# A two-layer boundary worked token tile by token tile: the last and the first four weight chunks, with norms, x pieces and transposes per tile

## The reference

```
y = sgu_mixer(h, ...)                          # ends with y @ w_out, K = 4096, N = 2048
x = x + gate * rms_norm(y, post_g[0])          # gate, scale, shift = cond @ ada_w + ada_b
h = rms_norm(x, pre_g[1]) * (1 + scale) + shift
cq, ckv, k_rope, z = jnp.split(h @ w_in, [448, 960, 1024], axis=-1)    # K = 2048
```

## Time and profile before

| | |
|---|---|
| median of three executions | 2643.91 us |
| profiled execution: time, span | 2648.92 us, 2647.1 us |
| mean granted clock of PE | 0.977 |
| PE busy | 2538.8 us (96%) |
| DVE busy | 1631.3 us (62%) |
| ACT busy | 1349.1 us (51%) |
| POOL busy | 424.9 us (16%) |
| DMA | 548.91 MB, mean 207 GB/s |

### The profile page before, as it was taken

One profiled execution on the slowest core, in us unless ns is written; L12 is line 12 of the kernel. 1 busy time (PEld: TensorE's weight loads), 2 busy tenths in 40 slices (PEclk: granted clock), 3 DMA queues, 4 the chain that ended last, 5 costly groups with the idle time before them and its releaser, 6 DMA issues.

```text
span 2647.1 us, 33773 instructions
## 1 busy us (share of the span) xinstructions
PE 2538.8 (96%) x11958; PEld 2098.1 (79%) x11958; DVE 1631.3 (62%) x2456; ACT 1349.1 (51%) x1845; POOL 424.9 (16%) x296
## 2 busy tenths in 40 slices
PE   4999999999996999997999999999999999999998
PEld 4788788888885888886778777878888888888887
DVE  7789887667765677755755555545555545545553
ACT  4555664444444455544467666644544444444443
POOL 0155463110020000010000000024110011110111
PEclk8999999999997999997999999989999999999999
DMA  9979877888773666653454545445555555565554
GB/s 345 331 264 341 272 250 256 273 286 282 250 272 110 202 203 203 211 184 110 154 167 152 174 153 165 149 153 179 187 191 191 185 195 184 185 195 183 185 184 140
DMA packets 363660, 548.91 MB, mean 207 GB/s; under 512 B 32300, under 2 KB 125840, under 8 KB 363152
## 3 DMA queue, kind: packets, MB, share of 16 engines
q1 hardware_dynamic: 361856, 541.37, 62.3%
q10 hardware_dynamic: 1680, 5.91, 0.6%
HBM read 545.13 MB, written 2.10 MB: 207 GB/s over the span
## 4 chain that ended last, share of the span: by engine, by line
PE 65%; DVE 2%; ACT 1%; issue 1%; POOL 0%; ACTq 0%; DVEq 0%; POOLq 0%
PE ps L1599 38%; PE ps L1604 19%; PE ps L1584 1%; PE ps L1586 1%; PE ps L1585 1%; PE ps L1827 1%; PE ps L1675 1%; PE ps L1826 1%; PE ps L1661 0%; PE ps L1649 0%; DVE tf L976 0%; DVE stage L1328 0%; PE ps L1927 0%; ACT hi L414 0%; PE ps L1926 0%
## 5 line engine op out<-in xcount | busy, mean ns | idle before, releaser
L868 DVE TENSOR_TENSOR lo<-raw,hi 128x1024 fp32r<-128x1024 f32 x838 | 1083.0, 1304 | 797.5 <-ACT hi L414 796.6
L414 ACT ACTIVATE hi<-raw 128x1024 fp32r<-128x1024 f32 x838 | 880.4, 1059 | 805.6 <-PE ps L1604 703.5
L1599 PE MATMUL ps<-hi,a_hi 128*128 128x512 f32 (+1 forms) x2208 | 877.2, 398 | 11.5 <-issue 4.7
L1599 PE MATMUL ps<-hi,a_lo 128*128 128x512 f32 (+1 forms) x2208 | 862.3, 391 | 0.0
L1604 PE MATMUL ps<-lo,a_hi 128*128 128x512 f32 (+1 forms) x2208 | 590.2, 390 | 3.0 <-DVE lo L868 3.0
L1599 PEld LDWEIGHTS ps<-hi,a_hi 128*128 128x128 f32 x2208 | 419.5, 190 | 102.0 <-issue 12.3
L1604 PEld LDWEIGHTS ps<-lo,a_hi 128*128 128x128 f32 x2208 | 415.5, 189 | 90.7 <-DVE lo L868 4.2
L1599 PEld LDWEIGHTS ps<-hi,a_lo 128*128 128x128 f32 x2208 | 419.6, 190 | 81.4
L1599 PE MATMUL ps<-hi,b_hi 128*128 128x512 f32 x1056 | 417.2, 395 | 1.7 <-DVE b_lo L952 1.4
L1599 PE MATMUL ps<-hi,b_lo 128*128 128x512 f32 x1056 | 412.7, 391 | 0.0
L1604 PE MATMUL ps<-lo,b_hi 128*128 128x512 f32 x1056 | 283.1, 390 | 0.0
(11 more groups left out here) (260 smaller groups left out, 1753.0 us busy)
## 6 DMA issues: line engine op xcount, KB each, us to landing
raw<-in_ada_w SPq DMA_DIRECT2D x96, 1024.0 KB
raw<-in_sgu_w_in SPq DMA_DIRECT2D x96, 1024.0 KB
raw<-in_w_up SPq DMA_DIRECT2D x64, 1024.0 KB
raw<-in_w_down SPq DMA_DIRECT2D x64, 1024.0 KB
raw<-in_w_in SPq DMA_DIRECT2D x42, 1024.0 KB
raw<-in_sgu_w_out SPq DMA_DIRECT2D x32, 1024.0 KB
raw<-in_w_in SPq DMA_DIRECT2D x128, 256.0 KB
raw<-in_mla_w_in SPq DMA_DIRECT2D x33, 512.0 KB
```

The source lines that it names most:

```text
L414: nc.scalar.activation(hi[:, q % CHUNKS, :], raw[:, r % RAWS, q % 2 * CW:(q % 2 + 1) * CW], ACT.Copy).then_inc(hi_ready, 1)
L868: nc.vector.tensor_tensor(lo[:, q % CHUNKS, :], raw[:, r % RAWS, q % 2 * CW:(q % 2 + 1) * CW], hi[:, q % CHUNKS, :].bitcast(F32), ALU.subt ...
L1599: nc.tensor.matmul(ps[:, 2 * s + t, 0:width], x[:, k0 + j, t * P:(t + 1) * P], hi[:, c, w], start=begins, stop=False)
```

## The change

In the second half of the last product the loop over blocks is written out. The fourth block's first-half sums are not copied to `y`: they stay in PSUM banks 2 and 3 (`stays`, `evicted=3`), and its second half is added to them there. The second of the four blocks uses banks 4 and 5 for that (`block_in(2)`). The fourth block's last four chunks are multiplied for tile 0 alone (24 matmuls), then for tile 1 alone (24 matmuls); `half_done` tells that tile 0 is complete, and the chunks count as used only as tile 1 is worked. The small matmuls of the conditioning vector stand behind them.

ACT squares the fourth block from PSUM, tile by tile (`act_tile_square`), and DVE multiplies it by the gate row (`dve_tile_gated`); POOL has three blocks instead of four. Each tile has its own two norms (`dve_tile_ss`, `act_tile_root`, `dve_tile_rstd`). x is updated, squared and scaled in pieces of 512 columns (`dve_x_update`, `act_x_square`, `dve_x_normal`). A transpose group is now four 128-column slices of one tile (`pe_quad`), taken in the order `QUADS`; scale and shift are on ACT, four instructions of 128 columns per group (`act_quad`), the remainder on DVE (`dve_quad`). In the second layer's first block, the first four chunks are multiplied for tile 0, then for tile 1, with the groups' transposes between them, and the last four for both. One root of a column of ones (`early`) stands before the fourth block, so that ACT's function table is loaded there. The core of the diff:

```diff
-            act_pairs_squared(act, n, None, y, raws=12)
-            act_root(act, n)
-            act_squares(act, n, lambda t: x[:, t, :], 0)
-            act_root(act, n)
-            act_split(act, n, 8, a_hi, modulated=True)
-
-            act_steps(act, n, 8)
...
+            nc.scalar.activation(early[:, :], ones[:, :], ACT.Sqrt)
+            act_steps(act, n, 5)
+
+            act.wait_ge(stage_free, n.stg.at(2))
+            act.wait_ge(half_done, 1)
+            act_tile_square(act, n, 0, 1)
+            act_tile_root(act, n, 0)
+            act_steps(act, n, 1)
+            for b in range(4):
+                act_x_square(act, n, 0, b, b + 1)
+            act.wait_ge(chunk_used, n.chunk.base + 2 + CHUNKS)
+            act_tile_square(act, n, 1, 1)
...
+            for i in range(2, 8):
+                act_quad(act, n, i, *QUADS[i], 1)
+                if i >= 4:
+                    act_steps(act, n, 1)
...
+        def act_quad(act, n, i, t, b, layer):
+
+            act.wait_ge(t_turned, n.tg.base + 1)
...
+                    ins = nc.scalar.activation(tf[:, i % 2, e * P:(e + 1) * P], bank, ACT.Identity,
+                                               bias=mod[:, layer, k:k + 1], scale=hscale[:, k:k + 1])
...
+                act.wait_ge(t_kept, n.kept.base)
+                ins = nc.scalar.activation(a_hi[:, 4 * b:4 * b + 4, to], tf[:, i % 2, :].rearrange("p (k s) -> p k s", k=4), ACT.Copy)
...
-            layer_out(dve, n, 0)
-            norm_x(dve, n)
-            layer_in(dve, n, 1)
+            dve_steps(dve, n, 5, ada=True)
+
+            n.bsq.base += 7
+            dve.wait_ge(block_sq, 2 + n.bsq.base)
+            dve_tile_ss(dve, n, 0, bss)
+            dve_tile_gated(dve, 0, 1, 2)
+            dve_tile_rstd(dve, n, 0)
...
+            for b in range(4):
...
+                dve_x_update(dve, 0, b)
+            dve_steps(dve, n, 1)
...
+            for i in range(2, 8):
+                dve_x_normal(dve, *QUADS[i])
+                if i >= 3:
+                    dve_quad(dve, n, i - 1, *QUADS[i - 1], 1)
+                    if i >= 5:
+                        dve_steps(dve, n, 1)
...
+QUADS = ((0, 0), (0, 1), (1, 0), (1, 1), (0, 2), (1, 2), (0, 3), (1, 3))
...
-            pe_pairs(pe, n, A, 2, ada=True, gate=True)
-            pe.wait_ge(n_out, 4)
-            pe_turn(pe, n, 8, cols(y), modulated=True)
...
+            for c in range(4):
+                pe_chunk(pe, n, A, 1, 2 * c, 2, NB, False, False)
+            pe_by_tiles(pe, n, A, 1, range(8, 16, 2), ends=True, tells=True)
+            n.acc.base += 2
+            columns()
...
+            quad(0)
+            quad(1)
+            pe.wait_ge(acc_free, n.acc.at())
+            pe_by_tiles(pe, n, A, 0, range(0, 8, 2), begins=True, before={
+                (0, 0): lambda: split(0), (0, 2): lambda: split(1), (0, 3): lambda: quad(2),
+                (1, 0): lambda: (quad(3), split(2)), (1, 1): lambda: quad(4), (1, 2): lambda: (quad(5), split(3)), (1, 3): lambda: quad(6)})
+            quad(7)
+            for c in range(4, 8):
+                if c % 2 == 0:
+                    split(c + 1)
+                pe_chunk(pe, n, A, 0, 2 * c, 2, NB, False, c == 7)
```

More of the change, by code:

```diff
@@ L1523, in _ @@
             pool.wait_ge(gate_kept, 1)
[L1524 to L1528, removed]
+            for b in range(3):
+                at = slice(b * NB, (b + 1) * NB)
+                pool_take(pool, n, lambda t: tt(y[:, t, at], y[:, t, at], stage[:, t, :], ALU.add))
+                gate(n, lambda: at)
+            n.bsq.base += 2
+            n.acc.base += 4
             n.acc.base += 4
@@ L1607, in pe_chunk, with pe_block @@
             n.chunk.base += 1
-        def pe_block(pe, n, x2, kts=KT, k0=0, step=2, width=NB, extra=None, place=lambda k: k):
+        def pe_block(pe, n, x2, kts=KT, k0=0, step=2, width=NB, extra=None, place=lambda k: k, ends=True):
             pe.wait_ge(acc_free, n.acc.at(2))
@@ L1613, in pe_block @@
             for c in range(kts // step):
-                pe_chunk(pe, n, x2, s, place(k0 + c * step), step, width, c == 0, (c + 1) * step == kts)
+                pe_chunk(pe, n, x2, s, place(k0 + c * step), step, width, c == 0, ends and (c + 1) * step == kts)
                 if extra and c in extra:
@@ L1680, in pe_blocks_turning, with pe_tile_chunk, pe_by_tiles, pe_quad @@
                     extra[6] = lambda: pe_ada(pe, n)
-                pe_block(pe, n, x2, extra=extra)
+                pe_block(pe, n, x2, extra=extra, ends=not (stays and b == 3))
             pe.wait_ge(t_lo, n.tg.base)
+        def pe_tile_chunk(pe, n, x2, s, k0, kts, width, t, ahead, begins, ends):
+            c = (n.chunk.base + ahead) % CHUNKS
+            out_ = ps[:, 2 * s + t, 0:width]
+            rows_ = slice(t * P, (t + 1) * P)
+            parts = [slice(j * (CW // kts), j * (CW // kts) + width) for j in range(kts)]
+            pe.wait_ge(hi_ready, n.chunk.at(ahead + 1))
+            for j, w in enumerate(parts):
+                nc.tensor.matmul(out_, x2[0][:, k0 + j, rows_], hi[:, c, w], start=begins and j == 0, stop=False)
+                nc.tensor.matmul(out_, x2[1][:, k0 + j, rows_], hi[:, c, w], start=False, stop=False)
+            pe.wait_ge(lo_ready, n.chunk.at(ahead + 1))
+            for j, w in enumerate(parts):
+                ins = nc.tensor.matmul(out_, x2[0][:, k0 + j, rows_], lo[:, c, w], start=False, stop=ends and j == kts - 1)
+            return ins
+        def pe_by_tiles(pe, n, x2, s, places, kts=2, width=NB, begins=False, ends=False, tells=False, before=None):
+            for t in range(T):
+                for c, k0 in enumerate(places):
+                    if before and (t, c) in before:
+                        before[t, c]()
+                    ins = pe_tile_chunk(pe, n, x2, s, k0, kts, width, t, c, begins and c == 0, ends and c == 3)
+                    if t:
+                        ins.then_inc(chunk_used, 1)
+                    if tells and c == 3 and t == 0:
+                        ins.then_inc(half_done, 1)
+            n.chunk.base += 4
+        def pe_quad(pe, n, i, t, b, out0, free, freed):
+            pe.wait_ge(n_out, out0 + i + 1)
+            if i >= 4:
+                pe.wait_ge(free, freed + i - 3)
+            for e in range(4):
+                k = 4 * b + e
+                ins = nc.tensor.transpose(ps[:, 4 + i % 4, e * P:(e + 1) * P], y[:, t, k * P:(k + 1) * P], ident)
+            ins.then_inc(t_turned, 1)
+            n.tg.base += 1
         def pe_gate_rows(pe, layer):
```

172 lines of the change are left out of this document (160 added, 12 removed).

## The result

The changed kernel takes **2625.82 us** (median of four executions, 2624.55 to 2628.95) beside 2644.12 us for the kernel before on the same chip (2643.72 to 2650.15): a ratio of 0.9927, 95% interval 0.9915 to 0.994, 18.3 us less. 2629.6 us was predicted, with a range of 2624 to 2641. The direction and the mechanism are as predicted; the gain at the boundary is 3 us larger than the 14.3 us of the sum.

The account below looks back on a forecast made before the run. PE was taken to bound the kernel, with 31.6 us idle at the layer boundary; the block ending at 842 instead of 856.29 gains 14.3 us, so 2643.91 - 14.3 = 2629.6 us, range 2624 to 2641.

Parts of the forecast that it names:

- DVE, not PE, starts the pass: Tile 0's first norm: square done at 796.2, DVE's last `ada_sum` at 795.95, or 797.4 with the shift.
- The x pieces: Tile 0's four x pieces on DVE: bounds 0.65 and 0.79 us each, taken 0.66, ending at 801.2.
- a scaling group on ACT: Scale and shift of one transpose group taken as 1.5 us, plus 0.63 for rounding: 2.15 us.
- six groups and four copies: ACT's queue for the second layer's first block: 16.9 us, from 816.4 to 833.3.
- The second of the rivals (given back): Behind the block, two late slabs of 5 us each would leave 4 us gained: 2640 us; chance 0.08.
- the ring's form that decides: Tile 1's groups as closed ring, 6.5 us a turn: up to 9 us lost; decides from about 5.9; chance 0.05.
- The shift by the early root: Fourth block: table load and root ahead of the `hi` copies shift DVE's work by 1.5 us at most.
- PE's wait for the remainder of chunk 4: Fourth block: remainder ends at 790.7, PE wants it at 789.4, so PE waits 1.3 us.
- The way to tile 1's first scaled piece: Tile 1's queued DVE work: last square on ACT at 814.4, first scaled piece at 815.7; PE waits 1.5 us.
- The margin: End of the second layer's first block: 840.9 by the sum, taken as 842 since hops counted 0.04 us.
- The first rival (low clock until 836): Tile-wise chunks at low clock until 836: block ends 846.4 to 847.6, 9 us gained, 2635 us; chance 0.12.
- The drain: ACT's table load: the skill's rule adds some 1380 ns; the prediction took 1.3 us in all, without it.

Follow-up runs that it names:

- last_both: Changed kernel with the first layer's last four chunks again multiplied for both tiles together: 2633.28 us, ratio 0.9955; boundary stretch 65.25 us.
- no_early: Changed kernel without the root of ones before the fourth block: 2627.71 us in one execution; boundary stretch 60.44 us.
- hoist_shared: Changed kernel with tile 1's scaled pieces directly behind its root and scale and shift of groups 3, 5, 7 on DVE: 2627.63 us, ratio 0.9925.
- squares_first_warm: Changed kernel with tile 1's squares ahead of tile 0's second group, no early root, plus twenty unused matmuls in PE's idle stretch: boundary stretch 57.47 us.
- warm: Changed kernel with twenty unused 512-column matmuls added in PE's idle stretch before the second layer's first chunk: boundary stretch 61.06 us.
- before: The kernel before the change, against which ratios are taken: 2644.12 us.

## Why the prediction came out as it did

The marks, in us from the start of the fourth block's chunk 4 (788.5 as the prediction worked it out, 782.40 in the profile after):

| step | predicted | measured |
|---|---|---|
| tile 0 done on PE | 6.8 | 5.9 |
| DVE done with the last `ada_sum` | 8.9 | 7.8 |
| tile 1 done on PE | 12.2 | 11.3 |
| second layer's first matmul | 19.6 | 18.1 |
| tile 1's first scaled piece done | 27.2 | 25.2 |
| second layer's tile 1 done | 39.7 | 37.9 |
| chunk 4 of that block | 41.6 | 39.3 |
| next block (taken 53.5) | 52.4 | 50.3 |

**Right.** DVE, not PE, starts the pass, and `last_both` put 4.2 us on that. The x pieces follow at 0.66 us (2.74 for four), a scaling group on ACT takes 1.51 + 0.63 = 2.14 us beside 2.15, six groups and four copies take ACT from 808.39 to 825.6, 17.2 us beside 16.9, with one pause of 0.85 us where none was forecast. No slab was late behind the block. The second of the rivals (given back) and the ring's form that decides did not occur.

**The shift by the early root was mis-sized: 1.5 us taken, 0.4 measured.** From the start of the stretch, DVE's preparation ended after 795.95 - 777.87 = 18.1 us before and 18.5 now. The root costs DVE 0.9 us by `no_early`, since 0.6 of 1.5 is paid back by the end of POOL's contention; and the squares and copies stand 0.4 us earlier on ACT where the loop is written out (782.35 - 777.87 = 4.48 us into the stretch before, 778.74 - 774.67 = 4.07 in `no_early`). PE's wait for the remainder of chunk 4, 1.3 us by the sum, is then 0.3 (the first two tile chunks take 3.00 us instead of 2 x 1.36). The prediction had the 1.15 us variance beside POOL in its rows and used it; it didn't ask which other DVE instructions POOL was slowing.

**The way to tile 1's first scaled piece was too long by another 0.5 us** (27.2 - 19.6 = 7.6 beside 25.2 - 18.1 = 7.1). I added DVE's remainders and ACT's squares one behind the other. In the trace ACT works from 797.52 to the end of the last square at 806.1 without a pause, DVE's two remainders lie beside it, and the norm begins when they are through, 0.3 us behind.

**The margin was wrong.** The sum gave 840.9, and I moved it to 842, the middle of the ends, for hops counted too short. No such hops show; without this the forecast would have been 1.1 us nearer. The last part, from tile 1's first piece to the next block, took 50.3 - 25.2 = 25.1 us beside 25.2 in the sum. The misses all have one sign: 1.1 us at the shift, 0.4 from there to the second layer's first matmul, 0.5 on the way to tile 1 and 1.1 in the margin, together about the 3 us by which the gain was forecast too small.

**The clock.** The first rival (low clock until 836) had something for it that the runs bear out elsewhere: behind waits the clock did fall in `hoist_shared` and `squares_first_warm`. In the changed kernel it was at full speed from 806 on. The row of 904 to 906 that spoke for it was read too narrowly: PE was busy in that window, but it had stood still for 3 us just before.

```profile
903.74 0.46 PE L1826 MATMUL ps<-y 128*128 128x128 f32 x2 [2.98 <-DVE y L1184]
```

The Trainium skill (TensorE: Matmul & The Clock Gate, HAM oscillation) describes a kernel throttled anew at each of its waits for DMA, which are longer than any wait of PE behind 806 here. The changed kernel doesn't test that, with waits of 1.16 and 1.65 us at a clock of 1.00; the stretch near 904 agrees, and in those two variants the clock fell once, behind shorter waits.

`warm` shows that the low clock at the start of the second layer cost nothing, though at it the first tile chunk takes 803.21 - 800.51 = 2.70 us instead of 1.36: the wait for tile 1 hides it.

**The drain.** The Trainium skill (ScalarE: Activation LUTs, What ACT_TABLE_LOAD costs) gives some 1380 ns of drain beside the load. In the changed kernel the load runs from 775.89 to 777.17 and the root begins at 777.18; in `no_early` it runs from 791.74 to 793.02 and the root begins at 793.04. The trace disagrees again.

Not settled: what of the 6.2 us by which the whole program before the boundary was earlier in one profile than in the other belongs to the change. The variants scatter as much with equal code, so I count it as scatter of single executions. The boundary's 17.3 us beside 18.3 us between the medians leaves 1.0 us, inside that scatter.

## What to carry to other kernels

Where one norm over whole rows stands between two products, split the tokens: one tile's product can then lie beside the other tile's norm. Find the engine that is continuously busy in the second tile's preparation and take from in front of it what is not needed yet: an order with tile 1's squares ahead of a group that PE wanted later, and its scaled pieces together, gave 4.9 us, while giving half of ACT's remaining groups' scaling to DVE, ahead of the remainders that PE waited for, lost 1.5. A slow clock is a cost only where nothing else is waited for; price it by adding unused matmuls, and look whether PE then runs into a wait that brings the clock down in a worse place.

## What the runs showed of the hardware

- A gap inside the work can cost more than a slow start: behind waits of 0.81 and 1.40 us (`squares_first_warm`) and behind one of 2.06 us (`hoist_shared`) the granted clock was 0.50 for a while; behind waits of 1.16 and 1.65 us in the changed kernel it was 1.00.
- Elementwise work of POOL and DVE on single precision at the same time slowed both (`before`, `no_early` against the changed kernel): 2.5 to 3.5 us for POOL's two products, 1.23 to 1.48 or 1.56 us for a 1024-column remainder, 0.75 to 1.11 us for a 512-column sum.
- Four 128-column instructions with scale and shift from PSUM take 1.36 us on DVE (`hoist_shared`) and 1.51 us on ACT: moving them bought nothing here.
